# Prompt attention without identity products: four score buffers, transposes two units behind, values three

## What is computed

```python
s = einsum('bqhd,bkhd->bhqk', q, k) * scale      # plus a bias or a causal mask
p = softmax(where(mask, s, -inf), axis=-1)
o = einsum('bhqk,bkhd->bqhd', p, v)
```

## Time and profile before

| | |
|---|---|
| time, median of 3 runs (lowest, highest) | 2556.54 us (2550.62, 2556.87) |
| the profiled execution | 2558.51 us, span 2556.8 us |
| mean granted clock of TensorE | 0.91 of 2.4 GHz |
| TensorE busy, VectorE, ScalarE, GpSimd | 82%, 47%, 25%, 37% of the span |
| first prompt attention | 97.50 to 148.63 us; TensorE busy 50.43 of 51.14, 128 identity instructions 22.62 |
| second prompt attention | 1351.60 to 1378.88 us; TensorE busy 23.75 of 27.28, 64 identity instructions 10.89 |

### The profile page before, as it was taken

The page is one execution under the profiler, slowest core; times in us unless marked ns, Lnnn a source line. Parts: engine busy times, 40 slices in busy tenths (PEclk is TensorE's granted clock), DMA queues, the critical chain, the costliest instruction groups (busy, mean ns, idle before and its releaser), DMA issues.

```text
span 2556.8 us, 37396 instructions
## 1 busy us (share of the span) xinstructions
PE 2106.9 (82%) x13993; PEld 1531.5 (60%) x13993; DVE 1198.0 (47%) x3472; ACT 633.0 (25%) x959; POOL 943.8 (37%) x844
## 2 busy tenths in 40 slices
PE   8887899999998666666678788999999996666666
PEld 3653589999996323333346235799999983323322
DVE  2442279713333433575257942699233333333332
ACT  1421115455552000000024341144555540000000
POOL 0001017870003655666203130059720016656564
PEclk9898999999999888888788898999999998888887
DMA  5425314444446999999701131434444459999998
GB/s 215 175 85 207 127 72 157 154 161 165 166 165 238 350 340 324 337 339 341 285 4 43 54 124 33 140 108 157 165 161 166 165 183 326 336 329 343 334 346 300
DMA packets 164885, 525.38 MB, mean 205 GB/s; under 512 B 20930, under 2 KB 37090, under 8 KB 164194
## 3 DMA queue, kind: packets, MB, share of 16 engines
q0 software_dynamic: 88064, 311.21, 34.2%
q1 hardware_dynamic: 76642, 211.79, 23.9%
HBM read 520.23 MB, written 2.69 MB: 205 GB/s over the span
## 4 chain that ended last, share of the span: by engine, by line
PE 59%; DMA 17%; POOL 9%; DVE 7%; issue 5%; ACT 2%; another core or an unknown queue 0%; SPq 0%; DVEq 0%; ACTq 0%; POOLq 0%; PEldq 0%
DMA v_slot<-in_peer_v,v_rows 15%; PE bank L636 15%; PE bank L788 10%; PE bank L790 9%; PE bank L789 9%; PE bank L847 8%; POOL v_slot L586 6%; POOL u_low L575 3%; PE bank L1099 1%; PE bank L842 1%; DVE s_turned L1519 1%; PE bank L662 1%; PE bank L656 1%; DVE s_tmp L2074 1%; DMA region<-in_cache_a_kt 1%
## 5 line engine op out<-in xcount | busy, mean ns | idle before, releaser
L586 POOL DMA_INDIRECT v_slot<-in_peer_v,v_rows x576 | 546.8, 949 | 790.3 <-PE bank L790 441.1
L788 PE MATMUL bank<-h_parts,u_high 128*128 128x288 f32 x2048 | 606.7, 296 | 6.3 <-POOL u_low L575 5.7
L789 PE MATMUL bank<-h_parts,u_high 128*128 128x288 f32 x2048 | 604.4, 295 | 0.0
L790 PE MATMUL bank<-h_parts,u_low 128*128 128x288 f32 x2048 | 602.7, 294 | 0.0
L847 PE MATMUL bank<-v_slot,weight_columns 128*32 128x512 f32 x2048 | 335.9, 785 | 278.2 <-DMA v_slot<-in_peer_v,v_rows 253.5
L575 POOL TENSOR_TENSOR u_low<-u_slot,u_high 128x1024 fp32r<-128x1024 f32 x120 | 320.8, 2683 | 370.3 <-ACT u_high L1290 370.3
L788 PEld LDWEIGHTS bank<-h_parts,u_high 128*128 128x128 f32 x2048 | 384.1, 188 | 9.6 <-POOL u_low L575 9.1
L790 PEld LDWEIGHTS bank<-h_parts,u_low 128*128 128x128 f32 x2048 | 385.8, 188 | 0.0
L789 PEld LDWEIGHTS bank<-h_parts,u_high 128*128 128x128 f32 x2048 | 384.6, 188 | 0.0
L1290 ACT CAST u_high<-u_slot 128x1024 fp32r<-128x1024 f32 x256 | 268.8, 1050 | 399.9 <-PE bank L790 245.8
L847 PEld LDWEIGHTS bank<-v_slot,weight_columns 128*32 128x32 f32 x2048 | 72.9, 127 | 405.3 <-issue 330.5
(11 more groups left out here) (341 smaller groups left out, 2167.8 us busy)
## 6 DMA issues: line engine op xcount, KB each, us to landing
u_slot<-in_peer_ut SPq DMA_DIRECT2D x256, 512.0 KB, 3.4
w_q<-in_peer_w_q SPq DMA_DIRECT2D x8, 2048.0 KB, 16.6
v_slot<-in_peer_v,v_rows POOLq DMA_INDIRECT x576
region<-in_ev_w_in SPq DMA_DIRECT2D x4, 2048.0 KB, 15.4
region<-in_cache_a_kt SPq DMA_DIRECT2D x8, 960.0 KB, 12.7
region<-in_cache_a_v SPq DMA_DIRECT2D x8, 960.0 KB, 14.8
region<-in_pool_kv POOLq DMA_DIRECT2D x32, 128.0 KB, 3.2
region<-in_pool_kv SPq DMA_DIRECT2D x32, 128.0 KB, 5.4
```

Source lines behind the costliest of these rows:

```text
L586: pool.indirect_dma_start(out=VS[n % NVS], out_offset=None, in_=v_rows, in_offset=bass.IndirectOffsetOnAxis(ap=IDX[:, t:t + 1], axis=0)).t ...
L788: pe.matmul(bank, uh, HR[:, 0, c, :], start=(c == 0), stop=False)
L789: pe.matmul(bank, uh, HR[:, 1, c, :], start=False, stop=False)
L790: ins = pe.matmul(bank, ul, HR[:, 0, c, :], start=False, stop=(c == KC - 1))
```

## The change

The probabilities take the place of the scores: the exponentials write into the tile that they read, which now has four buffers; the two buffers of probabilities are gone, and so SBUF use is the same. `fill` is gone. On TensorE step n issues scores of n, transposes of n-2, values of n-3; ScalarE copies the transposes of n-2 behind the exponentials of n; VectorE finishes unit n-3 behind `first(n)`, and `first(n)` waits for the copy of unit n-4 (`_pt`) instead of the exponentials of n-2. The maxima have four buffers too.

```diff
@@ TensorE, prompt_attention
-                def fill(bank):
-
-                    for _ in range(2):
-                        pe.matmul(bank[:, 0:P], ident, ident, start=True, stop=True)
-
                 def turn(n, u):
                     pair, qt = u
                     bank = to_act()
-                    fill(bank)
                     pe.wait_ge(sem(name + "_probs"), n + 1)
...
-                                               probs[:, n % 2, (hh * (qt + 1) + kt) * P:(hh * (qt + 1) + kt + 1) * P], ident)
+                                               probs[:, n % 4, (hh * (qt + 1) + kt) * P:(hh * (qt + 1) + kt + 1) * P], ident)
...
                 def values(n, u):
                     pair, qt = u
                     bank = to_dve()
-                    fill(bank)
                     pe.wait_ge(sem(name + "_pt"), n + 1)
...
-                for n in range(len(units) + 2):
+                for n in range(len(units) + 3):
                     if n < len(units):
                         scores(units[n])
-                    if 1 <= n <= len(units):
-                        turn(n - 1, units[n - 1])
-                    if n >= 2:
-                        values(n - 2, units[n - 2])
+                    if 2 <= n < len(units) + 2:
+                        turn(n - 2, units[n - 2])
+                    if n >= 3:
+                        values(n - 3, units[n - 3])
@@ ScalarE, exps_prompt
-                for n in range(len(units) + 1):
+                for n in range(len(units) + 2):
...
-                            ins = act.activation(dst[:, n % 2, hh * nk:hh * nk + nk], src[:, n % 2, hh * nk:hh * nk + nk], ACT.Exp,
-                                                 bias=MX[:, n % 2, hh:hh + 1], scale=scale, accum_out=SUMS[:, n % 4, hh:hh + 1])
+                            row = scores[:, n % 4, hh * nk:hh * nk + nk]
+                            ins = act.activation(row, row, ACT.Exp, bias=MX[:, n % 4, hh:hh + 1], scale=scale, accum_out=SUMS[:, n % 4, hh:hh + 1])
...
-                    if n >= 1:
-                        pair, qt = units[n - 1]
+                    if n >= 2:
+                        pair, qt = units[n - 2]
                         bank = full()
...
-                        copy_out(pt[:, (n - 1) % 2, 0:2 * (qt + 1), :].rearrange("p a b -> p (a b)"), bank[:, 0:w], name + "_pt")
+                        copy_out(pt[:, (n - 2) % 2, 0:2 * (qt + 1), :].rearrange("p a b -> p (a b)"), bank[:, 0:w], name + "_pt")
@@ VectorE, prompt_attention
-                    s = scores[:, n % 2, 0:2 * nk]
-                    if n >= 2:
-
-                        dve.wait_ge(sem(name + "_probs"), n - 1)
+                    s = scores[:, n % 4, 0:2 * nk]
+                    if n >= 4:
+
+                        dve.wait_ge(sem(name + "_pt"), n - 3)
...
-                for n in range(len(units) + 2):
+                for n in range(len(units) + 3):
                     if n < len(units):
                         first(n)
-                    if n >= 2:
-                        second(n - 2)
+                    if n >= 3:
+                        second(n - 3)
```

More of the change, by code:

```diff
@@ L183, in build @@
         TBL0 = r3.take(8, 768)
-        SP_ = r3.take(2, 512)
-        PP_ = r3.take(2, 512)
+        SP_ = r3.take(4, 512)
         r3.skip_to(0)
@@ L199, in build @@
         r2 = Carver(arena, R2_0, R2_N).skip_to(r2s + NORMED)
-        MX = r2.take(2, 2)
+        MX = r2.take(4, 2)
         SUMS = r2.take(4, 2)
@@ L293, in build @@
         W_OUT1 = [tile_at(f"w_out1_{n}", [KC, 512], at) for n, at in enumerate((HB[1], heads.at))]
-        S_D = heads.take("mla_scores", 2, 512)
-        P_D = heads.take("mla_probs", 2, 512)
+        S_D = heads.take("mla_scores", 4, 512)
         PT_D = heads.take("mla_probs_t", 2, 4, P)
@@ L917, in v0 @@
                 return Z[:, kt, col:col + HD]
-            prompt_attention(units0, "prompt0", q0, k0, v0, PP_, PTP)
+            prompt_attention(units0, "prompt0", q0, k0, v0, SP_, PTP)
             pe.wait_ge(sem("prompt0_done"), 16)
@@ L1077, in odd @@
                 prompt_attention(units, "prompt1", lambda h, qt: QCT[:, h, qt * P:qt * P + P], lambda h, nk: KCT[:, h, 0:nk],
-                                 lambda h, kt: VD[:, kt, h * HD:h * HD + HD], P_D, PT_D)
+                                 lambda h, kt: VD[:, kt, h * HD:h * HD + HD], S_D, PT_D)
                 pe.wait_ge(sem("prompt1_done"), 8)
@@ L1261, in tile_norms, with exps_prompt @@
                     act.activation(rinv[:, t:t + 1], rinv[:, t:t + 1], ACT.Sqrt).then_inc(sem("tile_rinv"), 1)
-            def exps_prompt(units, name, src, dst, scale):
-                for n in range(len(units) + 1):
+            def exps_prompt(units, name, scores, scale):
+                for n in range(len(units) + 2):
                     if n < len(units):
@@ L1338, in _ @@
             units0 = [(p, qt) for p in range(8) for qt in range(2)]
-            exps_prompt(units0, "prompt0", SP_, PP_, 1.0)
+            exps_prompt(units0, "prompt0", SP_, 1.0)
             for t in range(2):
@@ L1420, in odd @@
                 units = [(p, qt) for p in range(4) for qt in range(2)]
-                exps_prompt(units, "prompt1", S_D, P_D, SCALE_D)
+                exps_prompt(units, "prompt1", S_D, SCALE_D)
                 for t in range(2):
@@ L1548, in first @@
                     bank = full()
-                    s = scores[:, n % 2, 0:2 * nk]
-                    if n >= 2:
-                        dve.wait_ge(sem(name + "_probs"), n - 1)
+                    s = scores[:, n % 4, 0:2 * nk]
+                    if n >= 4:
+                        dve.wait_ge(sem(name + "_pt"), n - 3)
                     tables(s, bank, pair, qt, nk)
                     free()
-                    link(dve.tensor_reduce(MX[:, n % 2, :], s.rearrange("p (h k) -> p h k", h=2), AX, ALU.max, negate=True))
+                    link(dve.tensor_reduce(MX[:, n % 4, :], s.rearrange("p (h k) -> p h k", h=2), AX, ALU.max, negate=True))
                     if scale != 1.0:
-                        TS(MX[:, n % 2, :], MX[:, n % 2, :], scale, None, ALU.mult)
+                        TS(MX[:, n % 4, :], MX[:, n % 4, :], scale, None, ALU.mult)
                     say(name + "_scores")
```

## The result

The changed kernel took 2567.3 us in the median (2560.0 to 2573.7), the kernel before beside it 2556.7 (2550.6 to 2564.0): ratio 1.0039, 95% interval 1.002 to 1.0058. It is slower, by 10.6 us in the medians. The profiled execution took 2562.1 us with a span of 2560.4.

What follows compares the result with a forecast made beforehand. TensorE was taken to bound the first attention without a gap, a chain leaving it once per pair the second. Terms 8.3 + 3.5 + 0.7 = +12.5 us on the 2556.5 median gave 2569.0 us; 8-in-10 range 2555 to 2577.

Steps and rivals of the forecast that it cites:

- step 3: Both attentions: without identity products TensorE's clock stays at 0.50 throughout; cold in both given 0.62.
- step 1: TensorE per pair: removing identity products saves 1.8 us warm, 3.4 cold, leaving 3.96 warm or 7.2 cold.
- step 2: Values wait for ScalarE's copy behind the exponentials: warm loop 5.6 us in the first attention, 5.7 in the second.
- steps 4 and 5: Attention times at half clock: first +8.3 us (bounds 6 to 11), second +3.5 (bounds 1.5 to 6).
- so TensorE stays gapless: First attention cold: TensorE's 3.8 us of work covers the other engines' 3.4, so pairs cost 7.2 us.
- the 0.6 added for waits not followed: Second attention: allowance for waits not followed, raising the summed +2.9 us to +3.5.
- step 6: Stages behind the attentions: sample scores start cold again, +0.7 us, from a range of 0 to 3.
- The rival's reading of the Trainium skill: Both attentions: clock comes up as before, avoiding longer idle gaps being enough; pairs 5.6 us, time 2553.5; chance 0.16.
- plain cost: Both attentions: identity products were only cost, warm and no loop; 19.6 us less, 2537; chance 0.04.

Runs made afterwards that it cites:

- products back: Changed kernel with identity products put back into transposes and values, new order kept; attentions 51.3 and 26.7 us, ratio 1.0011.
- warm entry: Changed kernel with identity products only in TensorE's waits ahead of each attention, none inside; attentions 61.4 and 30.3 us, ratio 1.0073.
- thin products: Changed kernel, ScalarE copying before exponentials, identity products as before for four units, then one per unit; attentions 43.5 and 25.2 us, ratio 0.996.
- thin products in the first attention only: Copy-first kernel with one identity product per unit after the opening, but none there in the second attention; 46.2 and 24.7 us, ratio 0.9973.
- the changed kernel again: Changed kernel rerun unaltered against the kernel before; attentions 61.4 and 32.1 us, ratio 1.0077.

## Why the prediction was right, point by point

**The clock (step 3)** was right and was the whole case: 0.50 throughout both attentions, but for the first 0.7 us of the second. Two kernels that each change one side show it, products back (51.3) and products out of the old order (60.1).

**The products (step 1)**: the parting of a group behind scores into 0.45 of product and 0.19 of switch was right; without products the switch fell on the transposes, 0.62 for 0.43 and 1.04 for 0.85, that is 0.19 each at half clock too, where 0.30 had been assumed. TensorE's own cold pair, put at 7.2 us, is 7.16 where nothing waits.

**The loop (step 2)** was right in place and size, 5.69 us at full clock for 5.6, and in the second attention cold it is what a pair costs.

**The cold sums (steps 4 and 5)** came out too small, 8.3 for 10.3 and 3.5 for 4.8. The step that was mis-sized in the first is "so TensorE stays gapless". It set 3.8 us of TensorE's work against 3.4 of the other engines; measured from 119.80 to 123.42 it is 3.56 against 3.62. The wait of 0.06 looks like nothing, but with the values behind it (1.94 for 1.60) it costs 0.4, and it comes in five pairs, 2 us. The opening ahead of them was shorter than the sum had it, so that the last scores ended 51.8 us after the first ones, for 50.7. The rest is the drain, 9.6 us for 8.8: its two full values start behind a wait too, 1.94 and 1.96 for the 1.7 and 1.6 assumed, and the last copy isn't covered. The second sum is alike: its last full unit reached VectorE 1.0 us later than forecast, counted from the first scores (1359.9), and the drain took 9.8 us for 8.9; the 0.6 added for waits not followed covered a part. Its loop is 7.57, not 7.1, with the copy 1.24 us behind the first exponential (1.14 assumed), the values 0.73 behind the copy's start (0.63), and 1.94 long (1.7).

**What follows (step 6)** was put at +0.7 and is +0.2: cold from 160.0 to 169.2, but 4.8 us of that lie beside VectorE's spreading of the queries, and the sample scores ran cold for 4.4 us, against 3.4 before.

**The rivals.** The clock didn't come up by itself, in neither attention; in the two kernels in which it was up with the loop in place and no product inside, it fell (at 122.4 and at 1378.6 in the one with products in the opening; back and forth in the second attention of the warm entry). The rival's reading of the Trainium skill (TensorE: Matmul & The Clock Gate, "Why this matters for your kernels"), that avoiding longer gaps is enough, fails here: the clock fell at 122.4 with no gap longer than 1.64 us. Nor does leaving out all gaps bring it up: 56.36 of 56.50 us busy left it at 0.50. The first gain that the rival "plain cost" hoped for, a pair near 4 us, does exist, at 4.42, but only with the loop broken and the clock held.

**The total**: 2569.0 forecast, 2567.3 measured; that nearness is partly luck, since the attentions lost 3.3 us more than forecast (15.1 for 11.8), and the medians moved by 10.6 us in the first comparison and by 17.7 in the second, for 12.5 forecast.

## What to carry to other kernels

Work without a use can be what keeps TensorE's clock up: before taking it out, read the granted clock of the stretch and what the engine does that is left, and price the rest at half clock. Then look for loops through the other engines' queues: at full clock one makes idle time, and with it the clock fell here, so that moving a single copy ahead of two exponentials was worth 15 us. The buffers and the deeper order of this kernel helped only once ScalarE's queue issued the old unit's copy ahead of the new unit's exponentials.

## What the runs showed of the hardware

TensorE without a gap was not enough to raise its clock. In the first attention, whose scores fill 64 of 128 partitions and whose values are 64 columns wide, TensorE was busy 56.36 of 56.50 us at 0.50 and the clock stayed. With four identity products per unit (128 partitions, 128 columns) it came up 9.4 to 10.1 us after the first scores in five profiles (before, products back, thin products, both kernels with products in the opening only), and 15.4 us after them in a sixth (112.4, thin products in the first attention only).

In the second attention, with scores over 96 partitions, the clock rose three times behind 3.3 to 3.4 us without a gap and with no product near (warm entry, at 1376.6 and 1383.4; old order without products, at 1384.9). But it also stayed at 0.50 behind stretches of the same length, as gapless and with the same kind of work (old order without products, 1367.8 to 1371.2 and 1374.6 to 1378.0; the changed kernel again, 1356.8 to 1360.2). Which property of the work makes the difference stays open: no run changed the partitions or the columns alone.

Eight short f32 products behind a wait took longer than in a stream: 1.94 us for 1.60 at half clock, behind a wait of only 0.06 us, and 1.10 for 0.84 at full clock, behind one of 0.16. So a restart costs some 0.3 us, several times the wait.
